# Expert weights behind the output product: the second set in one piece, the third at the last stored rows

## What is computed

```python
mix = gates[:, :, 0] * y_gla + gates[:, :, 1] * y_dsa
out = mix @ w_out[l]
x = x + gate_m * rmsnorm(out, g_post_mix[l])
h = rmsnorm(x, g_pre_ffn[l]) * (1.0 + scale_f) + shift_f
y = hier_moe(h, ...)          # top-1 group, top-2 experts in it
x = x + gate_f * rmsnorm(y, g_post_ffn[l])
# in hier_moe, for each expert e: (silu(h w_g[e]) * (h w_u[e])) w_d[e]
```

## Time and profile before

| | |
|---|---|
| median of three runs | 853.93 us (849.37 to 855.02) |
| profiled execution, its own time | 853.91 us |
| its span, first to last instruction | 852.1 us |
| PE busy | 715.5 us (84%) |
| PE's mean granted clock | 0.927 |
| traffic over the span | 179.52 MB, mean 211 GB/s |

### The profile page before, as it was taken

The page is one execution under the profiler, slowest core; times in us unless marked ns, Lnnn a source line. Parts: engine busy times, 40 slices in busy tenths (PEclk is TensorE's granted clock), DMA queues, the critical chain, the costliest instruction groups (busy, mean ns, idle before and its releaser), DMA issues.

```text
span 852.1 us, 9690 instructions
## 1 busy us (share of the span) xinstructions
PE 715.5 (84%) x3475; PEld 445.1 (52%) x3475; DVE 377.2 (44%) x843; ACT 279.1 (33%) x503; POOL 104.7 (12%) x153
## 2 busy tenths in 40 slices
PE   2899989897897999989999999889887868777830
PEld 1336736575665767767787778643332323222310
DVE  3342225888997665653422747645211211121117
ACT  5223123643245767732122323222211211121123
POOL 3031302310000111000000001011110010010014
PEclk9999999998998899999999999969988999898985
DMA  9972492302202020022225462289999999999634
GB/s 342 392 272 99 149 345 100 107 17 83 99 1 100 1 89 12 1 100 99 72 76 177 169 247 98 92 311 422 420 421 419 421 419 420 420 420 420 255 149 174
DMA packets 45565, 179.52 MB, mean 211 GB/s; under 512 B 9566, under 2 KB 9672, under 8 KB 30156
## 3 DMA queue, kind: packets, MB, share of 16 engines
q1 hardware_dynamic: 37124, 149.48, 44.5%
q10 hardware_dynamic: 3464, 20.98, 6.7%
q0 software_dynamic: 4928, 8.42, 2.8%
HBM read 174.66 MB, written 12.59 MB: 220 GB/s over the span
## 4 chain that ended last, share of the span: by engine, by line
PE 67%; DVE 14%; issue 8%; DMA 5%; ACT 4%; SPq 0%; DVEq 0%; ACTq 0%; POOLq 0%
PE psA L477 10%; PE psA L479 9%; PE psA L478 9%; PE psG L849 8%; PE psS L849 7%; PE psA L870 7%; PE psA L469 4%; PE psT L836 2%; DVE mk_mem L1682 2%; DVE m L1681 2%; DVE arena_r L1648 2%; DMA gvs<-in_w_ada_dram 1%; PE psO L441 1%; DMA arena<-in_w_in_dram 1%; DVE qs_mem L1817 1%
## 5 line engine op out<-in xcount | busy, mean ns | idle before, releaser
L477 PE MATMUL psA<-arena_r 128*128 128x512 f32 x320 | 132.0, 413 | 1.6 <-DVE arena_r L1648 1.0
L478 PE MATMUL psA<-arena_r 128*128 128x512 f32 x320 | 127.7, 399 | 0.0
L479 PE MATMUL psA<-arena_r 128*128 128x512 f32 x320 | 127.3, 398 | 0.0
L1648 DVE TENSOR_TENSOR arena_r<-arena,arena_r 128x1024 fp32r<-128x1024 f32 (+1 forms) x31 | 59.9, 1950 | 46.1 <-ACT arena_r L1199 44.6
L849 PE MATMUL psG<-arena,kv 128*64 128x512 f32 x224 | 66.1, 674 | 14.1 <-issue 14.1
L477 PEld LDWEIGHTS psA<-arena_r 128*128 128x128 f32 x320 | 62.3, 195 | 23.6 <-issue 10.4
L849 PE MATMUL psS<-arena,kv 128*64 128x512 f32 x208 | 64.2, 667 | 12.1 <-issue 12.1
L479 PEld LDWEIGHTS psA<-arena_r 128*128 128x128 f32 x320 | 61.8, 193 | 13.7
L478 PEld LDWEIGHTS psA<-arena_r 128*128 128x128 f32 x320 | 62.2, 194 | 12.6 <-issue 0.5
L1199 ACT CAST arena_r<-arena 128x1024 fp32r<-128x1024 f32 (+1 forms) x31 | 49.8, 1628 | 26.1 <-DMA arena<-in_w_in_dram 15.3
L849 PEld LDWEIGHTS psG<-arena,kv 128*64 128x64 f32 x224 | 21.5, 154 | 45.5 <-issue 44.6
(11 more groups left out here) (382 smaller groups left out, 1241.5 us busy)
## 6 DMA issues: line engine op xcount, KB each, us to landing
arena<-in_w_e_gate_dram SPq DMA_DIRECT2D x27, 1024.0 KB, 24.8
arena<-in_w_e_up_dram SPq DMA_DIRECT2D x27, 1024.0 KB, 27.1
arena<-in_w_in_dram SPq DMA_DIRECT2D x11, 2048.0 KB, 8.0
arena<-in_w_e_down_dram SPq DMA_DIRECT2D x12, 1024.0 KB, 20.6
qs_mem<-in_w_e_down_dram SPq DMA_DIRECT2D x10, 1024.0 KB, 21.2
arena<-in_w_ada_dram SPq DMA_DIRECT2D x4, 2048.0 KB, 17.4
qT<-in_w_ada_dram ACTq DMA_DIRECT2D x8, 1024.0 KB, 5.1
gvs<-in_w_ada_dram ACTq DMA_DIRECT2D x8, 1024.0 KB, 5.9
```

The lines of the kernel that those rows point to most:

```text
L477: nc.tensor.matmul(acc, lhs[0], rhs[0], start=start, stop=False)
L478: nc.tensor.matmul(acc, lhs[0], rhs[1], start=False, stop=False)
L479: return nc.tensor.matmul(acc, lhs[1], rhs[0], start=False, stop=stop)
L1648: V.tensor_tensor(lo[:, part], src[:, part], hi[:, part], ALU.subtract).then_inc(lo_ready, 4 if q is None else 1)
```

## The change

Set 1 is loaded whole, by the function that the loop uses, as soon as the output product is complete. Set 2's loads wait for the last stored rows, and no longer for the first gather. No other engine's program changes.

```diff
             sp.wait_ge(ring_out, len(items))
-            gate_up(1, 0, 2)
-            down(1, 0, 2)
+            experts(1, 2, 3)
             sp.wait_ge(xn2_stored[1], 32)
-            down(1, 1, 3)
-            sp.wait_ge(xg_in[0], 16)
-            gate_up(1, 1, 3)
-
             gate_up(2, 0, 4)
             gate_up(2, 1, 5)
             down(2, 0, 4)
```

## The result

Over 22 runs each the changed kernel takes 859.33 us (median; 852.24 to 878.32) and the kernel before 854.81 (849.32 to 866.50). The ratio is 1.006, with a 95% interval from 1.0035 to 1.0084: slower by 3 to 7 us.

A forecast was written before the change was run, and what follows sets the result against it. The weight stream bounds the expert stage. Store and gather order +1.95, gather +5.4 and clock +0.5 delay the first down product by 7.85 us; less the 7.1 reserve, +0.75 us gives 854.7 us, range 849.5 to 860.0.

The forecast's parts named there:

- rival B: Store and first gather behind a full queue, 556 to 578 us, cost more than the reserve; up to 863.8; chance 0.20.
- reserve: Work left in the weight queue when pair 3's down loads are issued: 7.1 us of delay that costs the stream nothing.
- d: How much later the first down product ends, which releases pair 3's down loads; forecast 7.85 us.
- step 2: Last store of normalised rows, issued at 556.25 among six weight loads: 8.0 us to landing, not 3.9.
- step 3: GpSimd's first gather waits for that store instead of the routing tables: it goes 1.95 us later.
- step 4: The first gather enters a full weight queue and takes 8.9 us instead of 3.5: +5.4.
- step 5: TensorE idles longer before the expert rows, so half clock lengthens the first product: 0.5 us, bound 1.6.
- Step 1: Set 1 issued whole at 549: the hole at 558 to 570 us closes, worth at most 5.6 us of stream.
- Wrong if the first down product comes after 604: Sign for rival B; the forecast had the first down product end at 600, not 592.25.
- the case with half of each extra: Milder case of rival B: store 10.7, gather +6.8, clock 1.0; d 12.4, shift +5.3, 859.2 us.
- Rival A: Store waits once and passes whole, landing in 3.9 to 6 us; time 848.3 to 852.2; chance 0.17.
- Rival C: SyncE's queue is full and blocks the issues, so time stays 853.9; chance 0.03 together with others.

The follow-up runs named there:

- e10: The changed kernel, with five products that nobody reads added on TensorE while it waits for the first gather; 861.94 us, ratio 1.0086 to the kernel before.
- e3: The kernel before, with one VectorE step repeated 3 times between the first gate/up product and its act; 858.60 us against 855.47.
- e4: The kernel before, with one VectorE step repeated 9 times between the first gate/up product and its act; 862.43 us, ratio 1.0092.

## Why the prediction was right, and what was sized wrong

The mechanism and the range (849.5 to 860.0) held, and the time was within 1%: 859.33 us, where 854.7 was forecast. The size did not hold. The forecast was +0.75 us; measured are +3 to +7, and +3.8 in the profile, above the -1.7 to +3.6 that I gave a chance of 0.60 and in the lower part of rival B, to which I gave 0.20. That the sign came out right is partly luck: +0.75 was the difference of 7.85 and 7.1, and an error of 0.8 us in either would have turned it. The reserve was right. What was sized wrong is d, by its terms for the store and for the clock:

- **Store (step 2).** Taken 8.0, measured 9.2. The gather's penalty was carried over whole, and the store has twice its bytes. With a third of the traffic for 0.52 MB I had the 2.5 us at hand (2.9 measured); the 3.3 us of wait ahead of the first packet had no number of its own. It makes the gather go 3.2 us later (step 3), not 1.95.
- **First gather (step 4).** Taken +5.4, measured 8.54 - 3.48 = +5.1. Right.
- **Clock (step 5).** Taken 0.5 with a bound of 1.6, measured 1.0 in the first product and 1.6 in the turn before and in the first down product (601.16, 4.71 us). The bound was drawn over the first product alone. The second fall sits some 11 us behind it, where TensorE waits for VectorE, and appeared in the profile of every kernel in which d grew, e10 excepted; in the kernel before it was missing, though TensorE waits the same 1.4 us there. I had no term for it.
- **d.** 3.2 + 5.1 + 1.0 + 1.6 = 10.9 instead of 7.85.
- **Reserve.** 7.1, confirmed by e3 and e4 and by the line through five kernels. Shift = 10.9 - 7.1 = 3.8, as read.
- **Step 1.** Set 2 joined without a gap, 411 GB/s from 554 to 570. Two later holes opened, at 586 and 601; both had been named (585, and 597 to 602), with too short a second one. In them the stream lost (420 - 165) x 6 / 420 = 3.6 and (420 - 34) x 7 / 420 = 6.4 us, 10.1 together, against the 5.6 that the closed hole gave: 4.5 by this sum, and 3.8 read. The forecast had one hole of equal size come back.
- **What would show it.** "Wrong if the first down product comes after 604": it came 54.2 us after set 1's first load, which on the old axis is 603.2, 0.8 us short of that sign (in the changed kernel's own trace it is 605.9). B's mechanism is the forecast's with larger terms, and the result lies between the two, nearer to the case with half of each extra (+5.3).
- **Rival A** fell: the store didn't land in 3.9 to 6 us, and it didn't pass whole. It waited once, 4.1 us, and then its packets went one for one with the weights'. By the Trainium skill (DMA: Bandwidth & Descriptors, Queues, rings and completion order) a turn typically drains 9 to 17 descriptors of one queue; no run here shows such turns, and the packets 0.46 us apart speak against them.
- **Rival C** fell: no issue of set 2 took over 0.7 us.

## What to carry to other kernels

Where a stream of loads sets the time, a hole in it is worth closing only if the queue doesn't run dry later: ask which waits stand behind the hole, and read the reserve there from one landing on an empty queue and one at the wait in question. A small transfer on the critical path (a store that someone gathers, a gather that starts a stage) pays for the loads that are queued ahead of it. And loads go in the order in which they are used, with each wait in front of its own loads: the kernels with that order were 0.6 to 0.9% faster than the one before, and no placement of the first ones alone gained anything that the rounds could tell.

## What the runs showed of the hardware

- A 0.5 MB store took 2.6 us to land on idle DMA engines, and 3.6 to 3.9, 7.4 and 8.6 to 9.3 with three, four and six 1 MB loads issued 7 us ahead of it. Its first packet started 0.8 us after the issue on idle engines, and 1.6 to 1.7, 3.7 and 3.6 to 4.1 us after it with three, four and six loads. The first gather of 128 rows took 3.4 to 3.6 on idle engines and 8.0 to 9.1 behind full ones.
- Two full queues shared by packets, not by bytes: 156 to 140 packets, 1.15 to 0.52 MB, one by one.
- TensorE's granted clock was half while it waited for rows for some 10 us, and came back to full in the first product's first half; a pause of 1.4 us some 11 us later was followed by a second half-clock stretch in the change (601.16, 4.71 us) and by none in e10 (597.12, 3.58 us) and in the kernel before (588.66, 3.58 us).
